# Query, key and rotary chunks of the mixers computed with X's high and low part side by side in two bank pairs

## The chip, the cores and the metric

The kernel runs on one core of one Trainium2 chip. The metric is device time in microseconds (us) of that core for the whole two-layer decoder trunk. Three timed runs before the change gave 1534.26, 1534.9 and 1536.65 us, median 1534.9 us.

## The reference

There are 256 tokens of width 1024 and two layers. Each layer computes one combined input projection `x @ w_in` (17,408 columns), cut into queries, keys and values of three attention groups with 8 heads, queries, keys, values and gate of a 4-head retention, and two mixer gates. What the change touches is the part that makes queries and keys:

```python
proj = x @ w_in
# attention: three groups (window, dilation); all 8 heads of 128
scores = einsum(q, k) * 128 ** -0.5        # masked, softmax, times v
# retention: 4 heads, key width 256
q = rotary(q, positions);  k = rotary(k, positions) * 256 ** -0.5
# rotary: concatenate([t1 * cos - t2 * sin, t1 * sin + t2 * cos])
```

Everything is float32. The mixers' results go through projections (`w_attn_proj`, `w_ret_proj`, `w_out`), a layer norm, a per-layer embedding gate, a convolutional gated MLP (`w_up`, `w_down`) and a second layer norm.

## The kernel before, in words

**Arithmetic.** TensorE is given operands of type fp32r. The kernel splits each float32 operand into a high part (its rounding to fp32r) and a low part (the remainder), and a product is three matmuls: high by high, high by low, low by high. `xT_both` holds X transposed, for each of 8 blocks of 128 features the high part (256 tokens) and directly behind it the low part (256 tokens), so both parts of one block are 512 neighbouring columns.

**Chunks.** Weights are streamed in chunks of 256 output columns by 1024 inputs (1 MB, `CE` = 2048 elements per partition) through a ring of three buffers. For chunk c: SyncE loads `raw` once the low part of chunk c-3 has been formed (L256); ScalarE rounds it into `w_hi` once the matmuls of chunk c-3 are done (`to_hi`, L373); VectorE subtracts into `w_lo` (`to_lo`, L699); TensorE multiplies. ScalarE and VectorE prepare chunk c+2 at step c.

**A mixer iteration.** Each layer has four iterations `j` of 15 chunks (`C_MIX`), each with two attention heads and one retention head. Chunk 0 is a value chunk, 1 and 2 are retention values, 3 to 8 are query and key of the three attention groups, 9 and 10 are the retention's query and key (the rotary chunks), 11 and 12 are values, 13 and 14 are the retention's gate. Chunk c accumulates in PSUM bank c % 3 (banks 0, 1, 2, one at a time).

**Forms of the matmuls.** Chunks 3 to 10 use `transposed` (L1193 to L1203), that is `split_product` (L1184 to L1188): per block of 128 output columns (2) and block of 128 features (8) three matmuls of 256 columns each, 48 per chunk, all accumulating in one bank. The merge stage and the MLP already use `both_parts` (L1205 to L1217): a matmul of 512 columns (w_hi by X's high and low part side by side, L1212) and one of 256 columns (w_lo by the high part, into the second half, L1216), 16 + 16 per chunk. It needs two banks (a pair); the first half of each bank holds high by high, the second half the two cross terms, and ScalarE and VectorE add the halves.

**What follows a chunk.** ScalarE copies chunks 3 to 8 out of their bank into `qk` (`copy_out`, L381). For chunks 9 and 10 VectorE's `rotate` (L827 to L847) reads the bank in four products with cosine and sine (L836 to L840) and forms the rotated pair (L843, L844) in `roped`.

**Order.** Each engine runs its queue in the order written out by hand. At step c of a mixer ScalarE does `to_hi(c+2)`, then what belongs to chunk c; VectorE does `to_lo(c+2)`, then what belongs to c. At step 10 that is on ScalarE `to_hi(12)`, `exp(0)`; on VectorE `to_lo(12)`, `mask_and_max(0)`, `rotate(1)`. On TensorE `behind(c)` (L1348) puts small matmuls behind chunks: transposes behind 0, `attend` behind 2, attention scores behind 9 and 13, retention scores and transposes behind 12. Behind chunk 13 the retention's output goes to bank 3. `bank_free(c)` (L1336) is TensorE's wait for the previous reader of chunk c's bank; `USES`, `U_MERGE`, `U_PLE`, `U_MLP` count these readers. The merge stage begins right behind chunk 14 of the last mixer with `gate` on pair 0 (banks 0 and 1); it waits for the readers of both banks.

Of the kernel before, what the change touches and what calls it, by code (L numbers as in the profile page):

```python
# [15 lines left out]
F32 = mybir.dt.float32  # L16
# [44 lines left out]
CE_PLE = 2 * 512 + 2 * SEQ  # L61


USES = (20 + 8 + 2 + NF, 20 + 2, 20 + 8 + 2 + NF, 4 + 2)
U_MERGE = (20, 20, 20, 4)
U_PLE = (28, 20, 28, 4)
U_MLP = (30, 22, 30, 6)


VALUES = (1, 0, 11, (13, 14))  # L70


NB = 2 * D_FF // P
# [21 lines left out]
def program(nc, x, xT, positions, w_in, w_attn_proj, w_ret_proj, w_out, w_up, w_down,  # L95
            w_ple_gate, ple_operands, ln_rows, feature_params, constants, out):
    ctx = ExitStack()
    with ctx:
# [112 lines left out]
        exp_done, inv_ready, prob_ready = sem("exp_done"), sem("inv_ready"), sem("prob_ready")  # L211
        probT_done, probT_copied, pv_done = sem("probT_done"), sem("probT_copied"), sem("pv_done")
        attn_hi_ready, attn_lo_ready = sem("attn_hi_ready"), sem("attn_lo_ready")
        rope_products, roped_ready = sem("rope_products"), sem("roped_ready")
        rv_hi_ready = sem("rv_hi_ready")
        ret_scores_done, decayed_ready, ret_av_done = sem("ret_scores_done"), sem("decayed_ready"), sem("ret_av_done")
        decayed_hi_ready, decayed_lo_ready = sem("decayed_hi_ready"), sem("decayed_lo_ready")
# [15 lines left out]

        TAIL = C_MLP + 3 * (NF - 3) + 2
        R_LAYER = 16 * (C_LAYER // RING)

        def slot(l, c):

# [125 lines left out]
        def _(act):  # L364
# [58 lines left out]
            def mixer(l, j):  # L423
                it = l * NJ + j
                it2 = it * 2
                g = l * C_LAYER + j * C_MIX
                r = l * R_LAYER + j * (16 * C_MIX // RING)
                rv, v0, v12, g01 = VALUES
                one_by_one = l == 0 and j == 0
                tiles = tiles_before(l, j)  # L430

                def exp(a):
                    act.wait_ge(neg_max_ready, it2 + a + 1)
                    nc.scalar.activation(prob[:, 0:384], prob[:, 0:384], ACT.Exp, bias=neg_max[:, 0:1],
                                         accum_out=row_sum[:, 0:1])
                    nc.scalar.activation(prob[:, 384:1152], prob[:, 384:1152], ACT.Exp, bias=neg_max[:, 1:2],
                                         accum_out=row_sum[:, 1:2]).then_inc(exp_done, 1)

                def retention_scores():
                    copy_probT(0, it2 + 1)  # L440
                    act.wait_ge(decayed_ready, it + 1)
                    nc.scalar.activation(decayed_hi, decayed, ACT.Copy).then_inc(decayed_hi_ready, 1)

                for c in range(C_MIX):
                    if j or c:
                        to_hi(l, g, r, c + 2)
                    if one_by_one and c == 2:
                        act.wait_ge(angle_step, 10)
                        nc.scalar.activation(sinT[:, :], sinT[:, :], ACT.Sin).then_inc(rotary_ready, 1)
                        nc.scalar.activation(cosT[:, :], cosT[:, :], ACT.Sin).then_inc(rotary_ready, 1)  # L450
                    if j and c == 1:
                        finish_ret(l, j - 1, it, (bank[3], acc[3]))
                    if j and c == 3:
                        finish_attn(j - 1, it)
                    if c in (rv, rv + 1):
                        t = c - rv
                        if one_by_one:
                            act.wait_ge(chunk_done, g + c + 1 + RING)
                            nc.scalar.activation(rv_hi[:, :, t * CH:(t + 1) * CH],
                                                 bank[c][:, :].rearrange("p (t n) -> p t n", t=TT),  # L460
                                                 ACT.Copy).then_inc(rv_hi_ready, 1)
                        else:
                            if t == 0:
                                act.wait_ge(tile_done, tiles + 1)
                            else:
                                act.wait_ge(chunk_done, g + c + 1 + RING)
                            nc.scalar.activation(rv_hi[:, t, :], bank[c % 3][:, :], ACT.Copy).then_inc(rv_hi_ready, 1)
                    if c == v0:
                        copy_out(g, c, c % 3, att_v0[:, it % 2, :, :])
                    if c in range(3, 9):  # L470
                        copy_out(g, c, c % 3, qk[:, c - 3, :, :], scale=ATT_SCALE if c % 2 == 1 else 1.0)
                    if c == 10:
                        exp(0)
                    if c in (v12, v12 + 1):
                        t = c - v12
                        if t == 0:
                            act.wait_ge(tile_done, tiles + 1 + (not one_by_one))
                        else:
                            act.wait_ge(chunk_done, g + c + 1 + RING)
                        nc.scalar.activation(att_v12[:, :, t, :], bank[c % 3][:, :].rearrange("p (g n) -> p g n", g=2),  # L480
                                             ACT.Copy).then_inc(bank_read[c % 3], 1)
                    if c == 14:
                        exp(1)
                    for u in range(2):
                        if c == g01[u]:
                            copy_out(g, c, c % 3, silu[:, 2 * u:2 * u + 2, :], func=ACT.Silu)
                    if c == 12:
                        retention_scores()

# [199 lines left out]
        def _(dve):  # L689
# [130 lines left out]
            def mixer(l, j):  # L820
# [3 lines left out]
                rv, v0, v12, g01 = VALUES  # L824
                one_by_one = l == 0 and j == 0

                def rotate(i):  # L827

                    b = i
                    src = bank[b]  # L830
                    dve.wait_ge(chunk_done, g + 9 + i + 1 + RING)
                    if i == 0:
                        dve.wait_ge(rotary_ready, 2)
                        dve.wait_ge(ret_hi_ready, it + 1)
                    for h in range(2):
                        nc.vector.tensor_tensor(rope_c[:, h, :], src[:, h * SEQ:(h + 1) * SEQ], cosT[:, :], ALU.mult)  # L836
                    nc.vector.tensor_tensor(rope_s[:, 0, :], src[:, 0:SEQ], sinT[:, :], ALU.mult)\
                      .then_inc(rope_products, 1)
                    nc.vector.tensor_tensor(rope_s[:, 1, :], src[:, SEQ:2 * SEQ], sinT[:, :], ALU.mult)\
                      .then_inc(bank_read[b], 1)  # L840

                    dve.wait_ge(bank_read[b], l * USES[b] + j * 5 + 3 + 2)
                    nc.vector.tensor_tensor(roped[:, i, 0, :], rope_c[:, 0, :], rope_s[:, 1, :], ALU.subtract)  # L843
                    nc.vector.tensor_tensor(roped[:, i, 1, :], rope_s[:, 0, :], rope_c[:, 1, :], ALU.add)\  # L844
                      .then_inc(roped_ready, 1)
                    if i == 0:
                        dve.wait_ge(roped_ready, it2 + 1)  # L847
# [48 lines left out]
                for c in range(C_MIX):  # L896
# [9 lines left out]
                    if c in (rv, rv + 1):  # L906
# [5 lines left out]
                                                    rv_hi[:, :, t * CH:(t + 1) * CH].bitcast(F32), ALU.subtract)\  # L912
                              .then_inc(bank_read[c], 1)
                        else:
                            nc.vector.tensor_tensor(rv_lo[:, t, :], bank[c % 3][:, :], rv_hi[:, t, :].bitcast(F32),
                                                    ALU.subtract).then_inc(bank_read[c % 3], 1)
                    if c == 9:
                        rotate(0)
                    if c == 10:
# [258 lines left out]
        def _(pe):  # L1178
# [150 lines left out]
            def mixer(l, j):  # L1329
                it = l * NJ + j  # L1330
                it2 = it * 2
                g = l * C_LAYER + j * C_MIX
                used = [l * USES[b] + j * 5 for b in range(3)]
                rv, v0, v12, g01 = VALUES

                def bank_free(c):  # L1336
                    pe.wait_ge(bank_read[c % 3], used[c % 3] + c // 3 + 1)

                def scores(a):
                    for i in range(NG):  # L1340
# [7 lines left out]
                def behind(c):  # L1348
# [4 lines left out]
                    if j and c == 2:  # L1353
                        attend(it)
                    if c == 9:
                        pe.wait_ge(bank_read[2], used[2] + 4)
                        pe.wait_ge(attn_lo_ready, it2 + 2)
                        pe.wait_ge(ret_affine, it + 1)
                        scores(0)
# [9 lines left out]
                    if c == 13:  # L1369
                        pe.wait_ge(probT_copied, it2 + 1)  # L1370
                        scores(1)
                        pe.wait_ge(decayed_lo_ready, it + 1)
                        b = (rv + 1) % 3
                        pe.wait_ge(bank_read[b], used[b] + 2)
                        pe.wait_ge(bank_read[3], l * USES[3] + j + 1)

                        for o, (dst, t) in enumerate(((bank[3], 0), (acc[3], 0), (acc[3], 1))):
# [35 lines left out]
                for c in range(begin, C_MIX):  # L1413
                    if c in (rv + 1, v12 + 1):
                        behind(c)
                        continue
                    bank_free(c)
                    if c in (rv, v12):
                        weights_ready(g, c + 1)
                        two_chunks(l, c, c % 3, 0)  # L1420
                        bank_free(c + 1)
                        two_chunks(l, c, (c + 1) % 3, 1)
                    elif c == v0:
                        by_token(l, g, c, c % 3)
                        behind(c)
                    else:
                        transposed(l, g, c, c % 3, xT_hi, xT_lo)
                        behind(c)


# [193 lines left out]
```

## Time and profile before

| | |
|---|---|
| median of three timed runs | 1534.9 us |
| the profiled execution | 1534.09 us |
| its span, first to last instruction | 1532.3 us |
| TensorE busy | 1505.5 us, 9746 matmuls |
| weight loads busy (beside them) | 1375.5 us |
| VectorE / ScalarE busy | 963.8 us / 783.0 us |
| granted TensorE clock, mean | 0.997 |
| DMA | 265.85 MB, 173 GB/s |

The profile covers one execution. Its span is 1.8 us shorter than the time the same execution took. Durations of matmuls overlap (each is longer than the distance to the next start), so the cost of one is read from start to start.

### The profile page before, as it was taken

Reading aid. Unit: us, or ns where it says so; the run is one execution under the profiler, and the core shown is the slowest. Engines: PE = TensorE matmul, PEld = TensorE weight load, DVE = VectorE, ACT = ScalarE, POOL = GpSimd, SP = SyncE. Lnnn points to the kernel's source line nnn. Section 1 sums busy time; section 2 is a strip of 40 time slices with the busy share of each in tenths; the row PEclk is TensorE's granted clock in tenths of the full one; section 3 lists DMA queues with packets and bytes.
Section 4 is the critical chain, followed back from the end, with each engine's and each line's share of the span. In section 5 each row is a group of like instructions: output and inputs, shape, how many; then the busy total and the mean of one; then the engine's idle time right before and its main releaser. Section 6 shows DMA issues by size and latency. Waiting matters only on the chain.

```text
span 1532.3 us, 23024 instructions
## 1 busy us (share of the span) xinstructions
PE 1505.5 (98%) x9746; PEld 1375.5 (90%) x9746; DVE 963.8 (63%) x1079; ACT 783.0 (51%) x829; POOL 38.7 (3%) x23
## 2 busy tenths in 40 slices
PE   8999999999999999999999999999999999999997
PEld 8999999999988888888889999999999888878886
DVE  5564564745655587777765636556456556877777
ACT  5454463544644456556544645536446444556562
POOL 0000000000000010000000000000000000100000
PEclk9999999999999999999999999999999999999999
DMA  8544445445446564556455444454444565655560
GB/s 292 183 150 154 165 138 192 139 164 166 165 165 218 173 215 150 197 195 210 165 165 166 165 161 144 164 175 154 151 154 167 173 212 177 213 172 192 168 242 29
DMA packets 231479, 265.85 MB, mean 173 GB/s; under 512 B 4192, under 2 KB 221792, under 8 KB 230880
## 3 DMA queue, kind: packets, MB, share of 16 engines
q1 hardware_dynamic: 231248, 264.44, 51.5%
q8 instruction: 69, 1.13, 0.3%
q10 hardware_dynamic: 144, 0.13, 0.0%
q14 instruction: 18, 0.15, 0.0%
HBM read 263.50 MB, written 1.05 MB: 173 GB/s over the span
## 4 chain that ended last, share of the span: by engine, by line
PE 90%; DVE 7%; ACT 2%; issue 1%; DMA 0%; DVEq 0%; SPq 0%; ACTq 0%
PE bank L1212 18%; PE bank L1186 16%; PE bank L1188 16%; PE bank L1187 16%; PE bank L1216 9%; PE acc L1186 3%; PE acc L1187 3%; PE acc L1188 3%; DVE w_lo L699 3%; PE acc L1323 1%; PE acc L1344 1%; PE acc L1307 1%; DVE scratch L1061 1%; ACT w_hi L373 1%; PE acc L1341 1%
## 5 line engine op out<-in xcount | busy, mean ns | idle before, releaser
L699 DVE TENSOR_TENSOR w_lo<-raw,w_hi 128x2048 fp32r<-128x2048 f32 x241 | 551.8, 2290 | 400.7 <-ACT w_hi L373 400.4
L373 ACT ACTIVATE w_hi<-raw 128x2048 fp32r<-128x2048 f32 x243 | 463.2, 1907 | 166.6 <-PE bank L1188 108.4
L1186 PE MATMUL bank<-xT_both,w_hi 128*128 128x256 f32 x1312 | 373.9, 285 | 0.0
L1187 PE MATMUL bank<-xT_both,w_hi 128*128 128x256 f32 x1312 | 371.3, 283 | 0.0
L1188 PE MATMUL bank<-xT_both,w_lo 128*128 128x256 f32 x1312 | 371.3, 283 | 0.0
L1187 PEld LDWEIGHTS bank<-xT_both,w_hi 128*128 128x128 f32 x1312 | 251.8, 192 | 0.6
L1186 PEld LDWEIGHTS bank<-xT_both,w_hi 128*128 128x128 f32 x1312 | 251.7, 192 | 0.6
L1188 PEld LDWEIGHTS bank<-xT_both,w_lo 128*128 128x128 f32 x1312 | 251.7, 192 | 0.0
L1212 PE MATMUL bank<-xT_both,w_hi 128*128 128x512 f32 x928 | 234.8, 395 | 6.0 <-DVE w_lo L699 6.0
L1212 PEld LDWEIGHTS bank<-xT_both,w_hi 128*128 128x128 f32 x928 | 170.2, 191 | 37.8 <-issue 6.3
L1186 PE MATMUL bank<-w_hi,xT_both 128*128 128x256 f32 (+1 forms) x528 | 176.4, 334 | 5.0 <-DVE w_lo L699 1.8
L1188 PE MATMUL bank<-w_hi,xT_both 128*128 128x256 f32 (+1 forms) x528 | 175.1, 332 | 0.0
L1187 PE MATMUL bank<-w_lo,xT_both 128*128 128x256 f32 (+1 forms) x528 | 175.1, 332 | 0.0
L381 ACT ACTIVATE scratch<-bank 128x512 f32<-128x512 f32 x80 | 47.7, 597 | 217.0 <-PE bank L1188 216.7
L1216 PEld LDWEIGHTS bank<-xT_both,w_lo 128*128 128x128 f32 x928 | 126.6, 190 | 9.0
L1216 PE MATMUL bank<-xT_both,w_lo 128*128 128x256 f32 x928 | 129.4, 282 | 0.0
L1186 PEld LDWEIGHTS bank<-w_hi,xT_both 128*128 128x128 f32 x528 | 100.3, 190 | 16.6 <-issue 6.9
L1188 PEld LDWEIGHTS bank<-w_hi,xT_both 128*128 128x128 f32 x528 | 100.3, 190 | 9.5
L1187 PEld LDWEIGHTS bank<-w_lo,xT_both 128*128 128x128 f32 x528 | 100.4, 190 | 8.8
L1061 DVE SCALAR_TENSOR_TENSOR scratch<-scratch,feat 128x256 f32<-128x256 f32 x176 | 77.4, 481 | 40.1 <-ACT scratch L611 31.3
L1186 PE MATMUL acc<-w_hi,mid_hi 128*128 128x512 f32 x224 | 87.7, 392 | 0.3 <-DVE mid_lo L704 0.3
L1187 PE MATMUL acc<-w_lo,mid_hi 128*128 128x512 f32 x224 | 87.5, 390 | 0.0
(172 smaller groups left out, 1570.9 us busy)
## 6 DMA issues: line engine op xcount, KB each, us to landing
raw<-w_in SPq DMA_DIRECT2D x135, 1024.0 KB, 5.0
raw<-w_up SPq DMA_DIRECT2D x44, 1024.0 KB, 5.0
raw<-w_down SPq DMA_DIRECT2D x20, 1024.0 KB, 4.9
raw<-w_ret_proj SPq DMA_DIRECT2D x16, 1024.0 KB, 5.2
raw<-w_attn_proj SPq DMA_DIRECT2D x8, 1024.0 KB, 5.2
raw<-w_out SPq DMA_DIRECT2D x8, 1024.0 KB, 4.7
raw<-w_ple_gate SPq DMA_DIRECT2D x8, 1024.0 KB, 5.2
scratch<-ln_rows SPq DMA_DIRECT2D x4, 1024.0 KB, 7.8
```

The source lines that it names most:

```text
L373: nc.scalar.activation(w_hi[:, s, :], raw[:, s, :], ACT.Copy).then_inc(hi_ready, 1)
L381: nc.scalar.activation(dst, src, func, scale=scale).then_inc(bank_read[b], 1)
L699: nc.vector.tensor_tensor(w_lo[:, s, :], raw[:, s, :], w_hi[:, s, :].bitcast(F32), ALU.subtract).then_inc(lo_ready, 1)
L1061: ins = nc.vector.scalar_tensor_tensor(out=conv[:, 2 * half + b, :], in0=hpad[:, 2 * half + b, tap:tap + SEQ], scalar=feat[:, l, bass.ds(i ...
L1186: mm(dst, st_hi, mv_hi, start=start, stop=False)
L1187: mm(dst, st_hi, mv_lo, start=False, stop=False)
L1188: return mm(dst, st_lo, mv_hi, start=False, stop=stop)
L1212: mm(pair[p][:, m, :], hi[:, o:o + P], src[:, k0 + k, :, :].rearrange("p a t -> p (a t)"), start=first and k == 0, stop=False)
L1216: ins = mm(pair[p][:, m, SEQ:2 * SEQ], lo[:, o:o + P], src[:, k0 + k, 0, :], start=False, stop=last and k == KT - 1)
L1307: ins = nc.tensor.transpose(acc[i][:, o * P:(o + 1) * P], prob[:, src:src + P], ident)
L1323: mm(acc[a][:, 0:SEQ], v[:, 0, :], probT[:, a, i, 0:SEQ], start=(i == 0), stop=False)
L1341: mm(acc[0][:, i * P:(i + 1) * P], qk[:, 2 * i, a, 0:P], qk[:, 2 * i + 1, a, 0:P], start=True, stop=True)
```

## The change

Chunks 3 to 10 of every mixer go through `both_parts` on a pair of banks, chunk c on pair (c - 3) % 2: pair 0 is banks 0 and 1, pair 1 is banks 2 and 3. ScalarE copies the second halves (the cross terms) into `qk` or `roped`; VectorE then adds the first halves to them (`high_part`), with the attention scale, and releases the pair. `rotate` works from `roped` in SBUF in place of the bank. The other chunks keep one bank, by a new table: chunk 0 and 11 in bank 0, 1, 12 and 14 in bank 1, 2 and 13 in bank 2. The counters of bank readers are changed to match.

```diff
+BANK_READERS = ((0, 3, 5, 7, 9, 11), (1, 12, 14), (2, 4, 6, 8, 10, 13))
+        def bank_of(c):
+            return {0: 0, 1: 1, 2: 2, 11: 0, 12: 1, 13: 2, 14: 1}[c]
+        def pair_of(c):
+            return (c - 3) % 2
+        def reads_before(b, c):
+            return sum(i < c for i in BANK_READERS[b])
 # ScalarE, mixer, step c
-                    if c in range(3, 9):
-                        copy_out(g, c, c % 3, qk[:, c - 3, :, :], scale=ATT_SCALE if c % 2 == 1 else 1.0)
+                    if c in range(3, 11):
+                        act.wait_ge(chunk_done, g + c + 1 + RING)
+                        nc.scalar.activation(qk[:, c - 3, :, :] if c < 9 else roped[:, c - 9, :, :],
+                                             pair[pair_of(c)][:, :, SEQ:2 * SEQ], ACT.Copy,
+                                             scale=ATT_SCALE if c in (3, 5, 7) else 1.0).then_inc(mix_low, 1)
                     if c == 10:
                         exp(0)
 # VectorE, mixer
+                def high_part(c, dst, scale):
+                    b = 2 * pair_of(c)
+                    dve.wait_ge(mix_low, it * 8 + c - 3 + 1)
+                    nc.vector.scalar_tensor_tensor(out=dst, in0=pair[pair_of(c)][:, :, 0:SEQ], scalar=scale, in1=dst,
+                                                   op0=ALU.mult, op1=ALU.add).then_inc(bank_read[b], 1)
                 def rotate(i):
-                    b = i
-                    src = bank[b]
-                    dve.wait_ge(chunk_done, g + 9 + i + 1 + RING)
+                    b = 2 * pair_of(9 + i)
+                    src = roped[:, i, :, :]
+                    high_part(9 + i, src, 1.0)
...
+                    dve.wait_ge(bank_read[b], l * USES[b] + j * len(BANK_READERS[b]) + reads_before(b, 10 + i) + 1)
...
+                    if c in range(3, 9):
+                        high_part(c, qk[:, c - 3, :, :], ATT_SCALE if c % 2 == 1 else 1.0)
 # TensorE, mixer
                 def bank_free(c):
-                    pe.wait_ge(bank_read[c % 3], used[c % 3] + c // 3 + 1)
+                    b = 2 * pair_of(c) if c in range(3, 11) else bank_of(c)
+                    pe.wait_ge(bank_read[b], used[b] + reads_before(b, c) + 1)
+                    if c == 3:
+                        pe.wait_ge(bank_read[1], used[1] + reads_before(1, c) + 1)
+                    if c == 4:
+                        pe.wait_ge(ret_affine, it + 1)
...
+                    elif c in range(3, 11):
+                        both_parts(l, g, c, pair_of(c), xT_both)
+                        behind(c)
```

## Rows read from the trace of the kernel before

**Rows 1.** The page: busy by engine, granted clock by slice, chain by engine.

```profile
PE 1505.5 (98%) x9746; PEld 1375.5 (90%) x9746; DVE 963.8 (63%) x1079; ACT 783.0 (51%) x829; POOL 38.7 (3%) x23
...
PEclk9999999999999999999999999999999999999999
...
PE 90%; DVE 7%; ACT 2%; issue 1%; DMA 0%; DVEq 0%; SPq 0%; ACTq 0%
```

**Rows 2.** Waits of PE: who for whom, total us, times, longest.

```profile
PE bank L1212 <- DVE w_lo L699: 6.0, 2, 3.0
...
PE bank L1267 <- DVE stat L761: 1.6, 1, 1.6
PE acc L1293 <- DVE X L744: 1.4, 1, 1.4
```

**Rows 3.** Stretches: length, busy PE, PEld, DVE, ACT, POOL, clock, DMA share, GB/s.

```profile
30.53:70.85 40.32, 40.32 (x339) 40.32 (x337) 16.73 (x8) 16.88 (x14) 0.00 (x0) 1.00 0.61 198
...
449.82:477.73 27.91, 27.91 (x162) 24.57 (x161) 14.03 (x12) 12.18 (x10) 0.00 (x0) 1.00 0.60 202
```

**Rows 4.** Timeline of PE, merge stage: start, us, line, operation, count.

```profile
452.59 2.00 PE L1212 MATMUL bank<-xT_both,w_hi 128*128 128x512 f32 x8
...
455.38 2.00 PE L1212 MATMUL bank<-ret,w_hi 128*128 128x512 f32 x8
```

**Rows 5.** Timeline, first layer: end of the last mixer's chunk 14.

```profile
405.03 2.00 PE L1212 MATMUL bank<-xT_both,w_hi 128*128 128x512 f32 x8
...
405.23 0.60 ACT L381 ACTIVATE scratch<-bank 128x512 f32<-128x512 f32 x1 [1.72 <-PE bank L1188]
```

**Rows 6.** Timeline: how PE starts again after a wait for DVE.

```profile
18.94 0.36 PE L1186 MATMUL bank<-w_hi,xT_both 128*128 128x256 f32 x1 [0.26 <-DVE w_lo L699]
19.13 0.28 PE L1187 MATMUL bank<-w_lo,xT_both 128*128 128x256 f32 x1
...
16.50 2.29 DVE L699 TENSOR_TENSOR w_lo<-raw,w_hi 128x2048 fp32r<-128x2048 f32 x1 [1.00 <-ACT w_hi L373]
```

**Rows 7.** Timeline, second layer's first mixer: chunk 3, readers of chunks 1 and 2.

```profile
788.40 0.28 PE L1186 MATMUL bank<-xT_both,w_hi 128*128 128x256 f32 x1
...
787.78 0.68 DVE L915 TENSOR_TENSOR mid_lo<-bank,mid_hi 128x512 fp32r<-128x512 f32 x1
...
792.82 0.68 DVE L915 TENSOR_TENSOR mid_lo<-bank,mid_hi 128x512 fp32r<-128x512 f32 x1
```

**Rows 8.** Timeline of ACT and DVE behind one ordinary chunk (7) of a mixer.

```profile
252.25 0.60 ACT L381 ACTIVATE scratch<-bank 128x512 f32<-128x512 f32 x1 [3.37 <-PE bank L1188]
...
254.68 2.29 DVE L699 TENSOR_TENSOR w_lo<-raw,w_hi 128x2048 fp32r<-128x2048 f32 x1 [3.47 <-ACT w_hi L373]
```

**Rows 9.** Timeline of DVE and ACT behind chunks 9 and 10 of a mixer.

```profile
170.29 0.76 DVE L836 TENSOR_TENSOR scratch<-bank,cosT 128x256 f32<-128x256 f32 x2 [1.04 <-PE bank L1188]
172.28 1.28 ACT L434 ACT_TABLE_LOAD   x1
172.53 2.29 DVE L699 TENSOR_TENSOR w_lo<-raw,w_hi 128x2048 fp32r<-128x2048 f32 x1
177.90 0.62 ACT L434 ACTIVATE scratch<-scratch,stat 128x384 f32<-128x384 f32 x1 [4.34 <-DVE stat L864]
179.44 1.90 ACT L373 ACTIVATE w_hi<-raw 128x2048 fp32r<-128x2048 f32 x1
181.37 2.29 DVE L699 TENSOR_TENSOR w_lo<-raw,w_hi 128x2048 fp32r<-128x2048 f32 x1 [1.16 <-ACT w_hi L373]
184.11 0.61 DVE L871 TENSOR_SCALAR scratch<-scratch,stat 128x768 f32<-128x768 f32 x1
```

**Rows 10.** Timeline of PE: first matmuls of chunk 13 in that mixer.

```profile
190.93 0.36 PE L1186 MATMUL bank<-xT_both,w_hi 128*128 128x256 f32 x1
191.13 0.28 PE L1187 MATMUL bank<-xT_both,w_hi 128*128 128x256 f32 x1
```

**Rows 11.** Groups of DVE by line and form: busy us, mean ns.

```profile
L1049 DVE TENSOR_TENSOR scratch<-bank,scratch 128x512 f32<-128x512 f32 x42 | 28.9, 687 | 20.8 <-ACT scratch L604 20.8
L737 DVE SCALAR_TENSOR_TENSOR scratch<-scratch,stat 128x512 f32<-128x512 f32 x16 | 11.9, 783 | 0.0
```

More of the change, by code:

```diff
@@ L61 @@
 CE_PLE = 2 * 512 + 2 * SEQ
[L64 to L67, printed above, removed]
+USES = (24 + 8 + 2 + NF, 12 + 2, 24 + 8 + 2 + NF, 4 + 2)
+U_MERGE = (24, 12, 24, 4)
+U_PLE = (32, 12, 32, 4)
+U_MLP = (34, 14, 34, 6)
 VALUES = (1, 0, 11, (13, 14))
+BANK_READERS = ((0, 3, 5, 7, 9, 11), (1, 12, 14), (2, 4, 6, 8, 10, 13))
 NB = 2 * D_FF // P
@@ L213, in program @@
         attn_hi_ready, attn_lo_ready = sem("attn_hi_ready"), sem("attn_lo_ready")
-        rope_products, roped_ready = sem("rope_products"), sem("roped_ready")
+        mix_low, rope_products, roped_ready = sem("mix_low"), sem("rope_products"), sem("roped_ready")
         rv_hi_ready = sem("rv_hi_ready")
@@ L466, in mixer @@
                                 act.wait_ge(chunk_done, g + c + 1 + RING)
-                            nc.scalar.activation(rv_hi[:, t, :], bank[c % 3][:, :], ACT.Copy).then_inc(rv_hi_ready, 1)
+                            nc.scalar.activation(rv_hi[:, t, :], bank[bank_of(c)][:, :], ACT.Copy).then_inc(rv_hi_ready, 1)
                     if c == v0:
-                        copy_out(g, c, c % 3, att_v0[:, it % 2, :, :])
-                    if c in range(3, 9):
-                        copy_out(g, c, c % 3, qk[:, c - 3, :, :], scale=ATT_SCALE if c % 2 == 1 else 1.0)
+                        copy_out(g, c, bank_of(c), att_v0[:, it % 2, :, :])
+                    if c in range(3, 11):
[3 more added lines that the diff above has]
+                                             scale=ATT_SCALE if c in (3, 5, 7) else 1.0).then_inc(mix_low, 1)
                     if c == 10:
@@ L479, in mixer @@
                             act.wait_ge(chunk_done, g + c + 1 + RING)
-                        nc.scalar.activation(att_v12[:, :, t, :], bank[c % 3][:, :].rearrange("p (g n) -> p g n", g=2),
-                                             ACT.Copy).then_inc(bank_read[c % 3], 1)
+                        nc.scalar.activation(att_v12[:, :, t, :], bank[bank_of(c)][:, :].rearrange("p (g n) -> p g n", g=2),
+                                             ACT.Copy).then_inc(bank_read[bank_of(c)], 1)
                     if c == 14:
@@ L485, in mixer @@
                         if c == g01[u]:
-                            copy_out(g, c, c % 3, silu[:, 2 * u:2 * u + 2, :], func=ACT.Silu)
+                            copy_out(g, c, bank_of(c), silu[:, 2 * u:2 * u + 2, :], func=ACT.Silu)
                     if c == 12:
@@ L834, in rotate @@
                         dve.wait_ge(ret_hi_ready, it + 1)
+                    dve.wait_ge(bank_read[b], l * USES[b] + j * len(BANK_READERS[b]) + reads_before(b, 10 + i) + 1)
                     for h in range(2):
-                        nc.vector.tensor_tensor(rope_c[:, h, :], src[:, h * SEQ:(h + 1) * SEQ], cosT[:, :], ALU.mult)
-                    nc.vector.tensor_tensor(rope_s[:, 0, :], src[:, 0:SEQ], sinT[:, :], ALU.mult)\
+                        nc.vector.tensor_tensor(rope_c[:, h, :], src[:, h, :], cosT[:, :], ALU.mult)
+                    nc.vector.tensor_tensor(rope_s[:, 0, :], src[:, 0, :], sinT[:, :], ALU.mult)
+                    nc.vector.tensor_tensor(rope_s[:, 1, :], src[:, 1, :], sinT[:, :], ALU.mult)\
                       .then_inc(rope_products, 1)
-                    nc.vector.tensor_tensor(rope_s[:, 1, :], src[:, SEQ:2 * SEQ], sinT[:, :], ALU.mult)\
-                      .then_inc(bank_read[b], 1)
-                    dve.wait_ge(bank_read[b], l * USES[b] + j * 5 + 3 + 2)
+                    dve.wait_ge(rope_products, it2 + i + 1)
                     nc.vector.tensor_tensor(roped[:, i, 0, :], rope_c[:, 0, :], rope_s[:, 1, :], ALU.subtract)
@@ L914, in mixer @@
                         else:
-                            nc.vector.tensor_tensor(rv_lo[:, t, :], bank[c % 3][:, :], rv_hi[:, t, :].bitcast(F32),
-                                                    ALU.subtract).then_inc(bank_read[c % 3], 1)
+                            nc.vector.tensor_tensor(rv_lo[:, t, :], bank[bank_of(c)][:, :], rv_hi[:, t, :].bitcast(F32),
+                                                    ALU.subtract).then_inc(bank_read[bank_of(c)], 1)
+                    if c in range(3, 9):
+                        high_part(c, qk[:, c - 3, :, :], ATT_SCALE if c % 2 == 1 else 1.0)
                     if c == 9:
@@ L1332, in mixer @@
                 g = l * C_LAYER + j * C_MIX
-                used = [l * USES[b] + j * 5 for b in range(3)]
+                used = [l * USES[b] + j * len(BANK_READERS[b]) for b in range(3)]
                 rv, v0, v12, g01 = VALUES
                 def bank_free(c):
-                    pe.wait_ge(bank_read[c % 3], used[c % 3] + c // 3 + 1)
+                    b = 2 * pair_of(c) if c in range(3, 11) else bank_of(c)
[4 more added lines that the diff above has]
+                        pe.wait_ge(ret_affine, it + 1)
                 def scores(a):
@@ L1355, in behind @@
                     if c == 9:
-                        pe.wait_ge(bank_read[2], used[2] + 4)
+                        pe.wait_ge(bank_read[2], used[2] + reads_before(2, 9) + 1)
                         pe.wait_ge(attn_lo_ready, it2 + 2)
@@ L1372, in behind @@
                         pe.wait_ge(decayed_lo_ready, it + 1)
-                        b = (rv + 1) % 3
-                        pe.wait_ge(bank_read[b], used[b] + 2)
+                        b = bank_of(rv + 1)
+                        pe.wait_ge(bank_read[b], used[b] + reads_before(b, rv + 2) + 1)
                         pe.wait_ge(bank_read[3], l * USES[3] + j + 1)
@@ L1419, in mixer @@
                         weights_ready(g, c + 1)
-                        two_chunks(l, c, c % 3, 0)
+                        two_chunks(l, c, bank_of(c), 0)
                         bank_free(c + 1)
-                        two_chunks(l, c, (c + 1) % 3, 1)
+                        two_chunks(l, c, bank_of(c + 1), 1)
                     elif c == v0:
-                        by_token(l, g, c, c % 3)
+                        by_token(l, g, c, bank_of(c))
+                        behind(c)
+                    elif c in range(3, 11):
+                        both_parts(l, g, c, pair_of(c), xT_both)
                         behind(c)
                     else:
-                        transposed(l, g, c, c % 3, xT_hi, xT_lo)
+                        transposed(l, g, c, bank_of(c), xT_hi, xT_lo)
                         behind(c)
```

## The prediction

> **What bounds the kernel now.** I read the page first: TensorE is busy for 1505.5 of 1532.3 us at full clock in every slice (its upper level, 2.4 GHz), and the chain that ends last runs through it for 90% [rows 1]. VectorE with 63% and ScalarE with 51% have room. Next I read TensorE's waits: eight entries, from 6.0 us (two waits, at the MLP's start) to 1.4 us, 19.6 us together, and none of them in a mixer after the first loads [rows 2]. So in the mixers the time is the sum of the distances from one matmul's start to the next. For these distances I read the windows and the timeline. Seven `transposed` chunks in a row last 40.32 us, every engine of the matmul path busy throughout [rows 3]: 5.760 us a chunk, 120.0 ns for each of its 48 matmuls. Five `both_parts` chunks in a row last 27.91 us [rows 3]: 5.582 us a chunk. Half a chunk goes from 452.59 to 455.38, 2.79 us [rows 4], which confirms it.
>
> **The matmuls.** Both forms stream the same columns for a chunk: 48 x 256 = 12,288 before, 16 x 512 + 16 x 256 = 12,288 after. What goes is 16 matmuls, and 16 weight loads with them. The chunk falls by 5.760 - 5.582 = 0.178 us. Eight chunks in each of eight mixer iterations are 64: -11.4 us. Both ends of this price: 0.16 us if a longer first half behind small matmuls is charged to each iteration, or 0.18; that is -10.2 to -11.5 us. I take 0.175 and -11.2 us, since small matmuls interrupt the row of chunks twice in an iteration.
>
> **A wait at the merge stage.** Chunks 13 and 14 change places: 14 now sits in bank 1, and the merge stage's first `gate` wants banks 0 and 1. Before, bank 2 held chunk 14, and the gate began without a wait at 405.03, while ScalarE's Silu copy of chunk 14 ran from 405.23 for 0.60 us [rows 5]. Now the gate waits for that copy, until 405.83. From the end of the other engine's work to TensorE's next matmul it takes 0.15 us (w_lo ended at 16.50 + 2.29 = 18.79, the matmul began at 18.94), and the first matmul after a stop takes 0.19 us to the next instead of 0.12 [rows 6]. So 405.98 - 405.03 + 0.07 = 1.0 us for each layer, +2.0 us. Nothing else is queued ahead on TensorE; the engines behind it wait equally long. Bounds: 0 if the copy were not yet needed (no reason seen), 1.9 us a layer if the `w_hi` work queued behind the copy (1.90 us for a chunk, [rows 8]) should have to be waited for too, less the part that runs beside the gate.
>
> **A wait in the second layer.** Chunk 3 now needs bank 1 as well, whose reader is VectorE's low part of the retention values. In mixers with an iteration before them, `attend` lies between and hides it. In the second layer's first iteration nothing lies between: the reader ends at 787.78 + 0.68 = 788.46, chunk 3 began at 788.40 [rows 7]. So 788.61 - 788.40 + 0.07 = +0.3 us, once. Chunk 4 needs bank 2, read until 792.82 + 0.68 = 793.50 [rows 7]; it starts at 788.61 + 0.07 + 5.58 = 794.26, with 0.8 us to spare. Bank 3, which the previous iteration's retention used, has long been read.
>
> **ScalarE and VectorE behind an ordinary chunk.** ScalarE copies 512 columns as before (0.60 us) [rows 8]. VectorE adds `high_part`: not in the trace in this form, between the 687 ns of an addition from a bank and the 783 ns of a three-operand instruction of 512 columns [rows 11]; I take 0.69, since the multiply by a constant comes with an addition from a bank. It lies in the 3.47 us in which VectorE waits before each `w_lo` [rows 8], so it costs nothing. The pair is free 0.2 + 0.6 + 0.7 = 1.5 us after its chunk, and is wanted 5.58 us after it: 4.1 us of cover. SyncE's loads hang on `w_lo`, whose time behind ordinary chunks stays; the merge stage already draws 202 GB/s at the new pace, above the mixers' 198 [rows 3]. Without the cover each microsecond would cost 64.
>
> **Chunks 9 and 10.** Here the queues do move. Count from the end of chunk 9 at 170.09 (VectorE begins at 170.29). VectorE now waits for the copy until 170.9, adds 0.7, then does the six rotary operations, 2.24 us (170.29 to 172.53) [rows 9]: `w_lo` of chunk 12 begins at 173.9 instead of 172.53, and mask and maximum (ready at 177.9 before, by the exponential's start) end at 179.3. ScalarE's copy of chunk 10 stands ahead of `exp(0)` and its table load: chunk 10 ends at about 177.6, the copy at 178.4, the load (1.28) at 179.7. The exponential takes 1.54 us (177.90 to 179.44) [rows 9], to 181.2; `w_hi` of chunk 13 to 183.1; `w_lo` to 185.4, instead of 181.37 + 2.29 = 183.66. Chunk 13 starts at 190.93 [rows 10], about 190.7 after the change. So 5.3 us of the cover are left, and the load that waits for this `w_lo` has a whole chunk's time more than that. Normalising (it ended at 184.11 + 0.61 = 184.72, 1.1 us behind `w_lo` [rows 9]) ends at 186.5, and its transposes come 0.9 us before chunk 13. Cost: nothing; beyond 5 us of slip each further microsecond would cost 8.
>
> **Sum.** -11.2 + 2.0 + 0.3 = -8.9 us. The profiled execution took 1534.09 us, so 1525.2; from the median of three runs, 0.8 us above it, 1526.0 us. I forecast 1526.0.
>
> **Rivals.** (1) *Only columns count.* The 12,288 columns stay, and the saving does not appear in the mixers: 1534.9 + 2.3 = 1537.2 us, no difference that can be measured. For it: TensorE is fed the same data. Against it: the same two forms, with the same tiles, differ by 0.178 us a chunk in this very trace [rows 3]. The Trainium skill has a rule that leads there ("TensorE: Matmul & The Clock Gate", Back-to-back issue gap): the distance is N / 2.4 GHz plus about 2.5 ns. That gives an estimate of 5.24 us for 48 matmuls of 256 and 5.20 for 16 and 16, 0.04 us a chunk, 2.6 us in all, and a time within 1 us of now. The trace disagrees with it: 120.0 ns instead of 109 for 256 columns [rows 3], since each of these matmuls comes with its own weights. Chance 0.05.
>
> (2) *VectorE and ScalarE become the bound at chunks 9 to 11*, the other side. Mechanism: `high_part` and the copies hold up `w_lo` of chunk 13, and TensorE stands before it in each of the eight iterations. It decides from 5.3 us more slip than the 1.8 I have worked out. With 7.3 us more slip it costs 2 us x 8 = 16: 1526.0 + 16 = 1542 us, slower. For it: the two queues wait on one another three times between chunks 9 and 11, and the exponential now stands behind chunk 10. Against it: all durations are measured, and the cover is three times the slip. Chance 0.04.
>
> (3) *The waits do not show.* If the gate's wait ends with the last matmul, the gain is 11.2 us: 1523.7 us. Against it: the copy can't start before chunk 14 ends. Chance 0.04.
>
> (4) *Half the saving*: the long matmuls run in the mixers at a distance nearer to the two short ones, because two engines read the pairs more often. -5.6 + 2.3 = -3.3: 1531.6 us. Against it: in the merge stage the pairs are read in the same way. Chance 0.05.
>
> **How the numbers follow.** Forecast 0.82, its own range 1524.5 to 1527.5. A difference of 0.2%, 3.1 us, is about what a measurement here can tell from none: faster means below 1531.8, slower above 1538. Faster: 0.82 + 0.04 + half of (4) and a little of (1), 0.89; the same: 0.07; slower: 0.04. The range takes in rival 3 at its lower end, with the price of 0.18 us, 1523.3, and stops short of rival 4: 1523 to 1531.
>
> **What would show it.** Chunks 3 to 9 of a mixer as one block of 39.1 us instead of 40.3; 1024 matmuls more on the 512-column and on the 256-column line of `both_parts`, and 3072 fewer on the three of `split_product`; two waits for ScalarE's copy line of about 1 us at the first gates; one of about 0.2 us for VectorE's retention-value line in layer two; no wait for `w_lo` at chunks 11 to 14. Wrong: a `both_parts` chunk above 5.65 us in a mixer, or a repeated wait of TensorE in every iteration.

## The result, and the profile after

The changed kernel took 1526.0 us (median of 5 runs, 1524.87 to 1528.22), the kernel before, measured beside it, 1534.33 (5 runs). The ratio is 0.9947 with a 95% interval of 0.9933 to 0.9962: faster by 0.5%. On another chip five further runs gave 1524.86 against 1534.57 (9 runs of the kernel before), ratio 0.9934 (0.9921 to 0.9948). The profiled execution took 1525.84 us with a span of 1524.0, 8.3 us less than before.

The page of the changed kernel, with the group lines that answer to those of before; `both_parts` now stands at L1242 and L1246, the copy of the second halves at L490, `high_part` at L852:

```profile
PE 1495.9 (98%) x8722; PEld 1321.9 (87%) x8722; DVE 1007.8 (66%) x1143; ACT 792.3 (52%) x845; POOL 38.7 (3%) x23
...
L1242 PE MATMUL bank<-xT_both,w_hi 128*128 128x512 f32 x1952 | 492.9, 394 | 7.4 <-DVE w_lo L720 6.0
...
L1246 PE MATMUL bank<-xT_both,w_lo 128*128 128x256 f32 x1952 | 273.4, 283 | 0.0
...
L490 ACT ACTIVATE scratch<-bank 128x512 f32<-128x512 f32 x64 | 38.3, 598 | 227.0 <-PE bank L1246 227.0
...
L852 DVE SCALAR_TENSOR_TENSOR scratch<-bank,scratch 128x512 f32<-128x512 f32 x64 | 44.2, 691 | 87.1 <-ACT scratch L490 87.1
```

There are 1024 matmuls fewer than in [rows 1] (9746 to 8722), and weight loads are busy for 53.6 us less. VectorE has 64 additions more, at 691 ns each. ScalarE stands idle for 227.0 us ahead of its copies, all of it waiting for matmuls.

TensorE's waits (who for whom, total us, times, longest) are those of [rows 2] plus one entry, the gate's:

```profile
PE bank L1242 <- DVE w_lo L720: 6.0, 2, 3.0
...
PE bank L1242 <- ACT scratch L399: 1.4, 2, 0.7
```

The short wait at the second layer's chunk 3 has no entry of its own; it shows in the timeline below.

Windows of the changed kernel over chunks 3 to 9 of the first mixer of each layer, columns as in [rows 3]; below them TensorE's timeline at the first gate of each layer and at the second layer's chunk 3, with the reader of chunk 1:

```profile
30.56:69.66 39.10, 39.10 (x226) 34.40 (x225) 21.05 (x15) 16.93 (x14) 0.00 (x0) 1.00 0.62 205
784.32:823.51 39.19, 39.19 (x224) 34.48 (x225) 22.91 (x15) 18.62 (x15) 0.00 (x0) 1.00 0.66 215
```

```profile
399.48 0.28 PE L1218 MATMUL bank<-xT_both,w_lo 128*128 128x256 f32 x1
399.80 0.60 ACT L399 ACTIVATE scratch<-bank 128x512 f32<-128x512 f32 x1 [1.72 <-PE bank L1218]
400.45 2.12 PE L1242 MATMUL bank<-xT_both,w_hi 128*128 128x512 f32 x8 [0.69 <-ACT scratch L399]
402.41 1.11 PE L1246 MATMUL bank<-xT_both,w_lo 128*128 128x256 f32 x8
...
783.54 0.69 DVE L943 TENSOR_TENSOR mid_lo<-bank,mid_hi 128x512 fp32r<-128x512 f32 x1
783.93 0.39 PE L1218 MATMUL bank<-w_hi,xT_both 128*128 128x512 f32 x1
784.32 2.08 PE L1242 MATMUL bank<-xT_both,w_hi 128*128 128x512 f32 x8
786.25 1.11 PE L1246 MATMUL bank<-xT_both,w_lo 128*128 128x256 f32 x8
```

Seven chunks last 39.10 us instead of the 40.32 of [rows 3], 5.586 us each instead of 5.760. The gate would have begun at 399.60, 0.12 us behind the last start; it began at 400.45 and its first eight matmuls took 1.96 us instead of 1.84: 0.85 + 0.12 = 0.97 us. The copy had ended at 399.80 + 0.60 = 400.40, 0.05 us before. In the second layer the distance from 783.93 to 784.32 is 0.39 instead of 0.23 us, and the first eight matmuls took 1.93 us (784.32 to 786.25), 0.09 more: 0.25 us.

What a whole mixer iteration gained can be read between the same matmuls of two iterations, the attention scores behind chunk 9. First the kernel before, then the changed one:

```profile
170.09 0.83 PE L1341 MATMUL acc<-scratch 128*128 128x128 f32 x6
269.33 0.83 PE L1341 MATMUL acc<-scratch 128*128 128x128 f32 x6
```

```profile
167.54 0.83 PE L1376 MATMUL acc<-scratch 128*128 128x128 f32 x6
265.42 0.83 PE L1376 MATMUL acc<-scratch 128*128 128x128 f32 x6
```

An iteration took 99.24 us before and takes 97.88 now, 1.36 us less, or 0.170 us for each of its eight chunks. This is a little under the 0.174 of the undisturbed row, because the first eight matmuls of chunk 9, behind the scores, take 2.03 us instead of 1.84. Eight iterations give -10.9 us. The length of an iteration is also the steadier measure for the experiments: a span holds the start and two stops in the MLP, which differ from one execution to the next (last section).

### The profile page after: what moved, and what is told of

It is laid out like the page before. It is cut to its first block, busy times and chain, and to the rows that moved or that the text cites. A ratio compares the mean times of both kernels' runs of the same rounds, so it can differ in the third digit from the quotient of the medians.

```text
span 1524.0 us, 21056 instructions
## 1 busy us (share of the span) xinstructions
PE 1495.9 (98%) x8722; PEld 1321.9 (87%) x8722; DVE 1007.8 (66%) x1143; ACT 792.3 (52%) x845; POOL 38.7 (3%) x23
## 4 chain that ended last, share of the span: by engine, by line
PE 89%; DVE 7%; ACT 2%; issue 1%; DMA 1%; DVEq 0%; SPq 0%; ACTq 0%
PE bank L1242 34%; PE bank L1246 17%; PE bank L1216 8%; PE bank L1218 8%; PE bank L1217 8%; PE acc L1216 3%; PE acc L1217 3%; PE acc L1218 3%; DVE w_lo L720 3%; PE acc L1353 1%; PE acc L1379 1%; PE acc L1337 1%; DVE scratch L1091 1%; ACT w_hi L391 1%; PE acc L1376 1%
## 5 line engine op out<-in xcount | busy, mean ns | idle before, releaser
L1242 PE MATMUL bank<-xT_both,w_hi 128*128 128x512 f32 x1952 | 492.9, 394 | 7.4 <-DVE w_lo L720 6.0
L1242 PEld LDWEIGHTS bank<-xT_both,w_hi 128*128 128x128 f32 x1952 | 353.7, 189 | 73.2 <-issue 6.7
L1246 PEld LDWEIGHTS bank<-xT_both,w_lo 128*128 128x128 f32 x1952 | 267.7, 191 | 19.4
L1246 PE MATMUL bank<-xT_both,w_lo 128*128 128x256 f32 x1952 | 273.4, 283 | 0.0
L490 ACT ACTIVATE scratch<-bank 128x512 f32<-128x512 f32 x64 | 38.3, 598 | 227.0 <-PE bank L1246 227.0
L852 DVE SCALAR_TENSOR_TENSOR scratch<-bank,scratch 128x512 f32<-128x512 f32 x64 | 44.2, 691 | 87.1 <-ACT scratch L490 87.1
L1218 PE MATMUL acc<-w_hi,mid_lo 128*128 128x512 f32 x224 | 87.2, 389 | 0.0
L1216 PE MATMUL bank<-xT_both,w_hi 128*128 128x256 f32 x288 | 82.1, 285 | 0.0
L1217 PE MATMUL bank<-xT_both,w_hi 128*128 128x256 f32 x288 | 81.4, 283 | 0.0
L1218 PE MATMUL bank<-xT_both,w_lo 128*128 128x256 f32 x288 | 81.4, 283 | 0.0
L625 ACT ACTIVATE scratch<-bank 128x512 f32<-128x512 f32 x42 | 25.1, 597 | 103.0 <-PE bank L1246 103.0
```

The costliest lines, as they stand in the source:

```text
L490: nc.scalar.activation(qk[:, c - 3, :, :] if c < 9 else roped[:, c - 9, :, :], pair[pair_of(c)][:, :, SEQ:2 * SEQ], ACT.Copy, scale=ATT_SC ...
L625: nc.scalar.activation(hpad[:, 2 * half:2 * half + 2, 2:2 + SEQ], pair[half][:, :, SEQ:2 * SEQ], ACT.Copy).then_inc(up_low, 1)
L852: nc.vector.scalar_tensor_tensor(out=dst, in0=pair[pair_of(c)][:, :, 0:SEQ], scalar=scale, in1=dst, op0=ALU.mult, op1=ALU.add).then_inc(ba ...
L1216: mm(dst, st_hi, mv_hi, start=start, stop=False)
L1217: mm(dst, st_hi, mv_lo, start=False, stop=False)
L1218: return mm(dst, st_lo, mv_hi, start=False, stop=stop)
```

## The experiments

Each starts from the changed kernel ("after"). Spans are of the profiled execution.

**Splitting the long matmuls again.**

```diff
-mm(pair[p][:, m, :], hi[:, o:o + P], src[:, k0 + k, :, :].rearrange("p a t -> p (a t)"), ...)
+for q in range(2):                  # mixer chunks 3 to 10 only
+    mm(pair[p][:, m, q * SEQ:(q + 1) * SEQ], hi[:, o:o + P], src[:, k0 + k, q, :], ...)
```

> The changed kernel, but in mixer chunks 3 to 10 each matmul of 512 columns is issued as two of 256 (X's high part, then X's low part, same weights, same pair of banks). Columns, banks, copies and additions stay as in after; only the number of matmuls and weight loads goes back from 32 to 48 a chunk. My theory (a matmul costs a fixed part of about 11 ns beside its columns, because each has its own weight load): a chunk takes 5.76 us again instead of 5.586, the whole is 64 x 0.175 = 11.2 us longer than after, span near 1535. Rival (the columns count, and the gain comes from the banks or the order of the accumulation): a chunk stays at 5.59 us and the span at 1524. Rival (two matmuls in a row with the same weights are cheaper than with different weights): in between, under 1530.

> As the run with split matmuls, but only in chunks 3 to 6 (half of them). If the gain is a price for each matmul and nothing else, half of it is lost: 5.6 us more than after, span near 1529.6. If the gain hung on an uninterrupted series or on the pairs alone, all or nothing of it would go: 1535 or 1524.

Measured: with all eight chunks split, 1535.71 us (11 runs), ratio to the kernel before 1.0004 (0.9995 to 1.0013), span 1534.8; with four, 1531.27 (7 runs), 0.9972 (0.9961 to 0.9983), span 1530.6. The block of chunks 3 to 9 starts at 30.43 and ends at 70.75 in the first, 40.32 us as before; in the second it ends behind 39.80 us, at the attention scores:

```profile
70.27 0.83 PE L1381 MATMUL acc<-scratch 128*128 128x128 f32 x6
```

4 x 5.76 + 3 x 5.586 = 39.80. Banks, copies and additions were those of the changed kernel, and the whole gain of a chunk was gone. So the saving is a price for each matmul with its weight load, (5.760 - 5.586) / 16 = 10.9 ns here, and no matter of columns or banks. That both halves use the same weights did not make the second cheaper. With four chunks split the span is 6.6 us longer than in after instead of the expected 5.6, but 1.25 us of this lie behind the MLP's second stop, where TensorE's clock was low for longer. Two things stay open: every matmul here has a weight load of its own, so no run tells which of the two the 10.9 ns belong to; and they hold for this row of matmuls, not for any (six of the scores' 256-column matmuls take 1.11 us, 185 ns each, in after's trace).

**The gate's wait.**

```diff
-BANK_READERS = ((0, 3, 5, 7, 9, 11), (1, 12, 14), (2, 4, 6, 8, 10, 13))
+BANK_READERS = ((0, 3, 5, 7, 9, 12), (1, 11, 13), (2, 4, 6, 8, 10, 14))
-return {0: 0, 1: 1, 2: 2, 11: 0, 12: 1, 13: 2, 14: 1}[c]
+return {0: 0, 1: 1, 2: 2, 11: 1, 12: 0, 13: 1, 14: 2}[c]
+if c == 11:            # TensorE: pair 0 is released on bank 0's semaphore
+    pe.wait_ge(bank_read[0], used[0] + reads_before(0, c) + 1)
-pe.wait_ge(bank_read[b], used[b] + reads_before(b, rv + 2) + 1)    # behind chunk 13
+pe.wait_ge(bank_read[b], used[b] + reads_before(b, 11) + 1)
```

> The changed kernel (after) with the values' and gates' banks dealt out differently: chunk 11 in bank 1, 12 in bank 0, 13 in bank 1, 14 in bank 2, so that the merge stage's first gate (banks 0 and 1) needs only readers that finished early. My theory (the gate's wait for the Silu copy of chunk 14 costs 1.0 us a layer): the two waits of 0.69 us vanish, the first gate follows chunk 14 at the usual distance, and the span is about 1.9 us shorter than the after kernel's 1524.0, near 1522; no new wait elsewhere. Rival (the wait is only moved: something else is late at the merge stage, for instance the low part or a reader of bank 1): another wait of 0.5 to 1 us appears behind chunk 12 or 14 and the span stays at 1524. By the timed median either is within noise, the trace decides.

Measured: 1525.33 us (1520.91 to 1526.02), ratio to before 0.9934 (0.9921 to 0.9948), span 1519.1. The waits for L399 are gone, and the gate follows as expected. The list has one new entry, 0.2 us once for VectorE's `xT_both` (L774), which the repeat below does not have:

```profile
399.61 0.28 PE L1218 MATMUL bank<-xT_both,w_lo 128*128 128x256 f32 x1
399.73 2.00 PE L1242 MATMUL bank<-xT_both,w_hi 128*128 128x512 f32 x8
```

It starts 0.12 us behind the last matmul of chunk 14, 0.97 us a layer earlier than in after. That profile was shorter by 4.9 us, not 1.9; where the rest came from stands in the last section. By the medians the kernel is not told apart from after. So after and this kernel were timed again, beside each other on one chip:

> The changed kernel unchanged, on the same chip as the one with the re-dealt banks. Median near 1526, 8 to 10 us below before.

> The kernel with banks re-dealt (chunk 11 in bank 1, 12 in 0, 13 in 1, 14 in 2) again, beside after on the same chip. If the two gate waits are all that differs: 1.9 us below after's median. If the clock's drops at the MLP's start, which one profile of this kernel did not show, are rarer in it for good: 3 to 5 us below. If neither reaches the timed runs: the same.

Measured: after 1524.86 us (1524.34 to 1525.83), this kernel 1522.34 (1522.19 to 1525.05), before 1534.57; ratios to before 0.9934 (0.9921 to 0.9948) and 0.9925 (0.9911 to 0.9938). The medians differ by 2.5 us, near the 1.9 of two waits of 0.97, but the intervals overlap: the trace shows the gain, the timed runs alone do not prove it. The 1522.34 is the lowest median of the kernels run; on the first chip the same kernel took 1525.33.

**ScalarE's queue at step 10.** The exponential goes ahead of the copy of chunk 10.

```diff
+if c == 10:
+    exp(0)
 if c in range(3, 11):
     act.wait_ge(chunk_done, g + c + 1 + RING)
     nc.scalar.activation(...)                      # the copy
-if c == 10:
-    exp(0)
```

> The changed kernel with ScalarE's exponential of the first head ahead of its copy of chunk 10 instead of behind it, as the queue stood before. My theory: the position is worth nothing, since w_lo of chunk 13 has over 5 us of cover; span 1524 within 0.5 us and no new wait. What may change is that VectorE's addition for chunk 10 waits for the later copy by about 2 us. Rival (the queue behind chunk 10 is on the path): the span changes by 1 us or more in either direction.

Measured: 1525.39 us (4 runs), ratio 0.9939 (0.9924 to 0.9954), span 1522.9, no new wait. The span moved by 1.1 us, which by the rule above would speak for the rival. The trace speaks against it: a mixer iteration lasts 97.88 us as in after, and the 1.1 us are a drop of the clock behind the MLP's first stop that did not come here (1.54 us less), against a start that was 0.42 us later. VectorE's addition for chunk 10 waited for the copy, as expected:

```profile
179.40 0.69 DVE L852 SCALAR_TENSOR_TENSOR scratch<-bank,scratch 128x512 f32<-128x512 f32 x1 [2.18 <-ACT scratch L492]
```

**How much cover VectorE has at chunk 9.** The prediction gave 5.3 us, for `w_lo` of chunk 13. In after's trace something nearer is wanted. VectorE and TensorE of after, the second mixer: `w_lo` of chunk 12, then of 13, the end of normalising; the start of chunk 11 (with 12 in one block):

```profile
171.46 2.29 DVE L720 TENSOR_TENSOR w_lo<-raw,w_hi 128x2048 fp32r<-128x2048 f32 x1
...
180.68 2.29 DVE L720 TENSOR_TENSOR w_lo<-raw,w_hi 128x2048 fp32r<-128x2048 f32 x1 [1.02 <-ACT w_hi L391]
183.42 0.61 DVE L899 TENSOR_SCALAR scratch<-scratch,stat 128x768 f32<-128x768 f32 x1
...
175.10 0.40 PE L1216 MATMUL bank<-w_hi,xT_both 128*128 128x512 f32 x1
```

Three kernels put n = 4, 12 and 6 unused additions ahead of `high_part` of chunk 9 (shortened; two waits that keep the additions off data in use are left out):

```diff
 if c == 9:
+    for _ in range(n):
+        nc.vector.tensor_tensor(rope_s, mask[:, 0:2, :], mask[:, 0:2, :], ALU.add).then_inc(idle_done, 1)
+        dve.wait_ge(idle_done, ...)                # one after the other
     rotate(0)
```

> The changed kernel with four additions of 512 columns that nobody uses (each 0.68 us, and about 0.05 us until the next) on VectorE ahead of high_part of chunk 9, in every mixer iteration: VectorE's queue slips by about 2.9 us there. Theory A (as predicted: w_lo of chunk 13 decides, cover 5.3 us): span 1524, no new wait. Theory B (the normalised probabilities decide: they are ready at 184.03, their transposes begin at 187.32, cover 3.3 us): also 1524. Theory C (w_lo of chunk 12 decides: chunks 11 and 12 run as one block and both weights are wanted at 175.10, w_lo of 12 is ready at 173.75, cover 1.35 us): TensorE waits 1.5 us for w_lo ahead of chunk 11 in each of eight iterations, +12 us, span near 1536.

> The same with twelve such additions, a slip of 8.7 us. Theory A: (8.7 - 5.3) x 8 = +27 us, waits of TensorE for w_lo ahead of chunk 13. Theory B: (8.7 - 3.3) x 8 = +43 us, waits for the probabilities behind chunk 12. Theory C: (8.7 - 1.35) x 8 = +59 us, waits for w_lo ahead of chunk 11, nothing further behind it, span near 1583.

Measured: n = 4, 1529.47 us (5 runs), ratio to before 0.996 (0.9946 to 0.9974), span 1527.6 and no new wait listed; n = 12, 1587.93 us (one run), span 1584.9, with the wait ahead of chunk 11:

```profile
PE bank L1226 <- DVE w_lo L721: 47.9, 11, 5.8
```

n = 4 fitted none of the three. About two of its additions ran in time that VectorE had spare before the copy of chunk 9 was done (`w_lo` of chunk 11 done at 169.06, chunk 9 at 169.80, and `high_part` due 0.83 us behind it): the queue slipped by 1.3 us, not 2.9. `w_lo` of 12 then ended at 175.03 + 2.29 = 177.32, just as chunk 11 was due, which cost 0.2 us an iteration (98.08 instead of 97.88), 1.6 in all; the other 2 us of its span lie before 32.6 us, in the start. n = 12 came within 2 us of theory C's 1583, and its wait is where C put it, but the sum is right by luck: the stop was 5.77 us in each iteration, not 7.35, because of the same 1.6 us of spare time, and behind the stop TensorE's clock was at its lower level, which cost 1.85 us more (last section). The third run was put with the slip corrected:

> Six unused additions (0.72 us apart, 4.3 us) ahead of high_part of chunk 9. The run with four showed that 1.6 us of them fall into VectorE's own idle time ahead of the end of chunk 9, so that its queue slipped by 1.3 us and TensorE lost 0.2 us in each iteration. Theory C (w_lo of chunk 12, cover 1.35 us), with that slip: 4.3 - 1.6 = 2.7 us of slip, 1.4 to 1.5 us in each of eight iterations, +11 to +12 us, span 1535 to 1536 (2 us more if the start is late as in the run with four). Theories A and B (cover 5.3 or 3.3 us): none, 1524 to 1526.

Measured: 1537.34 us (one run), span 1535.5, +11.5. Waits of TensorE, then the timeline around chunk 11:

```profile
PE bank L1226 <- DVE w_lo L721: 13.1, 11, 1.4
```

```profile
178.08 0.47 PE L1226 MATMUL bank<-w_hi,xT_both 128*128 128x512 f32 x1 [1.41 <-DVE w_lo L721]
...
168.21 4.32 DVE L854 TENSOR_TENSOR scratch<-const 128x512 f32<-128x512 f32 x6
172.56 0.69 DVE L861 SCALAR_TENSOR_TENSOR scratch<-bank,scratch 128x512 f32<-128x512 f32 x1
...
175.64 2.29 DVE L721 TENSOR_TENSOR w_lo<-raw,w_hi 128x2048 fp32r<-128x2048 f32 x1
```

Eleven waits, 13.1 us; three of them are the 1.9 us that after has at other places, the eight others 1.4 each. Chunk 11 starts 1.57 us later than it was due (0.95 us behind 175.56, the start of the last eight matmuls of chunk 10), and its first matmul takes 0.08 us more: an iteration lasts 99.53 us, 1.65 more than in after, or 13.2 in all. The +11.5 of the span, inside the expected +11 to +12, is smaller because the start was 0.24 us earlier and one drop of the clock in the MLP (1.56 us) did not come. `w_lo` of chunk 12 decides, with 1.35 us of cover.

**VectorE behind ordinary chunks.** The same additions, n = 3 and n = 6, ahead of `high_part` in each of chunks 3 to 8.

> The changed kernel with three such additions (2.2 us) ahead of high_part in each of chunks 3 to 8. The prediction gave 4.1 us of cover for releasing the pair. VectorE's own work there is then 2.29 + 0.69 + 2.2 = 5.2 us a chunk, below the chunk's 5.59. Both theories (release of the pair decides; VectorE's sum decides): no cost, span 1524, no new waits.

> The same with six additions (4.35 us) in each of chunks 3 to 8. If the release of the pair decides alone, with 4.1 us of cover (in the trace of after the pair is released 1.3 us behind its chunk, so 4.3): waits of at most 0.3 us a chunk, up to +15 us. If VectorE's sum decides, 2.29 + 0.69 + 4.35 = 7.3 us a chunk against 5.59: the slip grows by 1.7 us a chunk, 10 us over six chunks, less what cover there is at chunk 12 (1.35 us): about 8.5 us in each of eight iterations, +60 to +75 us, span 1584 to 1600.

Measured (one run each): n = 3, 1524.25 us, span 1522.5, no new wait and 97.88 us an iteration, with 94.5 us more work on VectorE (the span is shorter than after's by one missing drop of the clock, 1.56 us). n = 6, 1577.17 us, span 1575.2, +51.2. TensorE's waits:

```profile
PE bank L1254 <- DVE scratch L863: 31.1, 27, 1.3
PE acc L1388 <- DVE scratch L863: 10.4, 8, 1.3
```

Neither theory held as it was put. VectorE's sum sets the pace: `high_part` (L863 here) starts every 7.15 us, and once the slip has used up its cover so do TensorE's chunks, with a stop of 1.3 us in each. In 27 cases TensorE waits for the release of the pair. In the eight others it waits for the sum itself: L1388 are the attention scores behind chunk 9, which read what `high_part` made of chunk 8, a consumer that neither the prediction nor these theories had listed. The list has no new wait for `w_lo`; the additions stop at chunk 8.

## Why the prediction was right

- *Matmuls*: predicted 5.582 us a chunk, measured 5.586. Of the -11.2 us predicted, -10.9 came (1.36 us in each of eight iterations); the 0.170 us a chunk lie within the bounds of 0.16 and 0.18 that the prediction gave, and the lower value has the reason it named, small matmuls ahead of chunk 9. Splitting the matmuls back gave it all back.
- *Gate*: predicted 1.0 us a layer, measured 0.97; re-dealing the banks removed it. The two parts were off in opposite directions: TensorE started 0.05 us behind the copy, not 0.15, and its first eight matmuls lost 0.12 us, not 0.07.
- *Second layer, chunk 3*: predicted 0.3 us, measured 0.25.
- *ScalarE and VectorE behind ordinary chunks*: predicted free with 0.69 us for the addition, measured 691 ns and no wait. n = 3 and n = 6 show that the cover is real and ends. For work repeated in every chunk the limit is not the prediction's 4.1 us but VectorE's spare time, 5.59 - 2.29 - 0.69 = 2.6 us, between the 2.2 that cost nothing and the 4.3 that cost. Whether 4.1 us hold for a single slip was not tried.
- *Chunks 9 and 10*: predicted free, and free. But its bound failed: "beyond 5 us of slip each further microsecond would cost 8". The step looked only at `w_lo` of chunk 13 and passed over that of chunk 12, which is wanted at the start of chunk 11, because the two run as one block. Its own numbers had it: `w_lo` of 12 from 173.9, done at 176.2, and chunk 10's end at 177.6. The cover was 1.35 us, and rival 2 decided from a quarter of the slip that I gave it. Here nothing came near it.
- *Readings of the profile before*: the shortest of the eight waits is 1.3 us, not 1.4. And the clock was not full throughout: the page's slices of 38 us hide a drop behind each of the MLP's two stops, as the mean of 0.997 hints.
- *Sum*: -8.9 us predicted; -8.3 between the two spans and between the medians on the first chip, -9.7 on the second. The trace accounts for the -8.3: -10.9 for the matmuls, +1.94 for the gates, +0.25 for chunk 3, and +0.43 because the clock's two drops in the MLP cost 3.09 us in after and 2.66 before. That the median came out at just the 1526.0 forecast is luck: the forecast starts from 1534.9, the five runs beside it gave 1534.33.
- *Rivals*: (1) fell with the block of 39.10 us. The Trainium skill's rule ("TensorE: Matmul & The Clock Gate", Back-to-back issue gap), which its section gives for a single isolated matmul, would gain 0.04 us a chunk; measured are 0.174 in the undisturbed row. (3) fell with the gate's wait, (4) with the 5.586 us.

## What to carry to other kernels

When the matrix engine is never idle, count its instructions and read the distance between their starts for each form: two forms that stream the same columns can differ, and a stage that already uses the new form gives its length to 0.1%. When banks or buffers are dealt out anew, walk across the seam to the next stage too, for the first user there may want one whose reader is late. And to bound a cover, list every consumer that waits behind the delayed queue: two chunks that run as one block want both weights at the start of the first, and a result can be read as data while its buffer is not yet wanted. A run that lands on the forecast span can still do so by two errors; a length inside the loop tells.

## What the runs showed of the hardware that was not expected

At the MLP's start TensorE stops for 3.00 us for `w_lo`, in every kernel here. In some executions the granted clock then falls to its lower level (1.2 GHz, 0.5) and in others not: behind the two stops it fell twice in before's profile and in after's, once in after's repeat, never in the first run with re-dealt banks and once in its repeat. The stretch from 590 to 606 us in after and in the first run with re-dealt banks, columns as in [rows 3]:

```profile
590.00:606.00 16.00, 13.00 (x59) 10.88 (x59) 13.27 (x17) 9.75 (x12) 0.00 (x0) 0.89 0.58 199
```

```profile
590.00:606.00 16.00, 13.62 (x70) 11.70 (x71) 14.17 (x17) 11.29 (x13) 0.00 (x0) 1.00 0.59 199
```

The first half chunk behind the stop takes 4.43 us (593.23 to 597.66) in after and 2.87 (592.38 to 595.25) in the other: 1.56 us. Between 1338 and 1362 us the clock was 0.93 in after and 1.00 in the other. The second drop cost 1.54 us, the two together 3.1. With the two gate waits (1.9), less a start that was 0.1 us later, they are the 4.9 us by which the two spans differ. In the run with twelve additions, whose stops last 5.8 us, the clock was 0.50 from 188.9 to 192 us, and the block behind it took 12.76 us instead of 10.91. So in these runs a stop followed by such a drop cost 1.3 to 2.8 us more than its length (1.31 at the second stop of before, 2.79 at that of the run with four chunks split), and the five executions of one kernel, the re-dealt banks, have spans from 1519.1 to 1523.7 us. What decides whether the clock falls behind a stop of 3 us was not tried.
